# Routing work moved into VectorE's waits, own buffers for the sample's rows, a deeper last stage, two up accumulators

## What is computed

```
x = x + gt1 * (concat(a_out, b_out) @ w_out)      # b_out = y * sigmoid(y @ w_glu + b_glu)
h = rms_norm(x, g_norm2) * (1 + sc2) + sh2        # shift, scale, gate: one row per sequence
g_prob = softmax(h @ w_group + b_group);  g_idx = argmax       # 4 groups
e_logits = h @ w_expert + b_expert                              # 32 experts, 8 in a group
e_top, e_idx = top_2 of the 8 logits in the chosen group
gate = g_w * softmax(e_top)
x = x + gt2 * sum_k gate_k * (silu(h @ w1[e_k]) * (h @ w3[e_k])) @ w2[e_k]
y = rms_norm(x, g_final)
```

## Time and profile before

| | us |
|---|---|
| median of 3 runs | 1870.66 (1867.41 to 1872.51) |
| the profiled execution's own time | 1870.08 |
| its span, first to last instruction | 1868.4 |
| busy in the span: PE, DVE, ACT, POOL | 1449.6, 1007.3, 568.4, 701.0 |

### The profile page before, as it was taken

The page is one execution under the profiler, slowest core; times in us unless marked ns, Lnnn a source line. Parts: engine busy times, 40 slices in busy tenths (PEclk is TensorE's granted clock), DMA queues, the critical chain, the costliest instruction groups (busy, mean ns, idle before and its releaser), DMA issues. The chain is left out here.

```text
span 1868.4 us, 26204 instructions
## 1 busy us (share of the span) xinstructions
PE 1449.6 (78%) x6641; PEld 1086.6 (58%) x6642; DVE 1007.3 (54%) x2144; ACT 568.4 (30%) x976; POOL 701.0 (38%) x545
## 2 busy tenths in 40 slices
PE   3891899999859999398888886189999999994000
PEld 0140688888635666177777775168788887883000
DVE  3993756556355330335445553468555585761567
ACT  1121422323120000211111211068554485661232
POOL 0841223232115320023433333237443365563664
PEclk9996899999965555599999998589999999997555
DMA  4756311111181001634333342489976599985674
GB/s 117 267 181 219 113 68 45 67 57 61 36 164 40 18 6 69 233 115 166 136 135 135 149 149 73 155 276 372 359 270 244 207 370 363 325 313 184 215 276 161
DMA packets 165677, 322.78 MB, mean 173 GB/s; under 512 B 21677, under 2 KB 93421, under 8 KB 164952
## 3 DMA queue, kind: packets, MB, share of 16 engines
q1 hardware_dynamic: 150426, 276.20, 43.1%
q0 software_dynamic: 13664, 45.70, 7.1%
q10 hardware_dynamic: 1536, 0.26, 0.1%
HBM read 235.74 MB, written 86.39 MB: 172 GB/s over the span
## 5 line engine op out<-in xcount | busy, mean ns | idle before, releaser
L2022 POOL TENSOR_TENSOR down_lo<-expert_raw,down_hi (+1 forms) x64 | 157.1, 2476 | 180.9 <-ACT down_hi L2114 180.9
L2161 DVE TENSOR_TENSOR up_lo<-expert_raw,up_hi (+1 forms) x128 | 170.4, 1372 | 21.0 <-ACT up_hi L2109 20.2
L619 PE MATMUL ps_up<-up_hi,xT_hi 128*128 x400 | 161.8, 405 | 4.5 <-DVE up_lo L2161 2.9
L621 PE MATMUL ps_up<-up_hi,xT_lo 128*128 x400 | 157.2, 393 | 0.0
L620 PE MATMUL ps_up<-up_lo,xT_hi 128*128 x400 | 156.6, 392 | 0.0
L2109 ACT ACTIVATE up_hi<-expert_raw (+1 forms) x128 | 125.3, 1057 | 3.5 <-DMA expert_raw<-in_w 1.7
L619 PE MATMUL ps_out<-wout_hi,catT_hi 128*128 128x512 f32 (+1 forms) x272 | 109.0, 401 | 2.7 <-DVE catT_lo L1607 2.7
L621 PE MATMUL ps_out<-wout_hi,catT_lo 128*128 128x512 f32 (+1 forms) x272 | 107.5, 395 | 0.0
L620 PE MATMUL ps_out<-wout_lo,catT_hi 128*128 128x512 f32 (+1 forms) x272 | 107.4, 395 | 0.0
L448 PE MATMUL ps_ada<-wada,cT 128*9 128x512 f32 x192 | 87.7, 615 | 10.9 <-DMA wada<-in_w_ada 5.8
L782 POOL TENSOR_TENSOR v<-v,lng 128x512 f32<-128x512 f32 (+1 forms) x17 | 21.9, 1290 | 194.6 <-DVE v L931 194.6
(11 more groups left out here) (363 smaller groups left out, 3571.4 us busy)
## 6 DMA issues: line engine op xcount, KB each, us to landing
expert_raw<-in_w SPq DMA_DIRECT2D x96, 1024.0 KB
expert_rows<-yo SPq DMA_DIRECT2D x49, 512.0 KB
wada<-in_w_ada SPq DMA_DIRECT2D x12, 2048.0 KB
x<-in_x_prompt SPq DMA_DIRECT2D x32, 512.0 KB, 3.6
expert_rows<-blank SPq DMA_DIRECT2D x31, 512.0 KB, 4.1
x_rows<-x SPq DMA_DIRECT2D x16, 512.0 KB, 2.6
moe_in_rows<-h SPq DMA_DIRECT2D x16, 512.0 KB
x<-x_rows SPq DMA_DIRECT2D x16, 512.0 KB
```

The lines of the kernel that those rows point to most:

```text
L619: pe.matmul(out, left(0, k), right(0, k), start=k == 0, stop=False)
L621: last = pe.matmul(out, left(1, k), right(0, k), start=False, stop=k == n - 1)
L2022: pool.tensor_tensor(down_piece(down_lo, run, m), raw_piece(run, 2, m, 1), down_piece(down_hi, run, m).bitcast(F32), ALU.subtract).then_in ...
L2161: dve.tensor_tensor(up_piece(up_lo, run, m), raw_piece(run, m // 2, m % 2, KD // 2), up_piece(up_hi, run, m).bitcast(F32), ALU.subtract).t ...
```

## The change

1. `mixout`, VectorE: `select(n-1)` now stands in odd steps between `bias_z` and `gated(i,1)`; `ranks(n-2)` in even steps between `low_y` and `gated(i,0)`; `slots(n-2)` in even steps between `bias_z` and `gated(i,1)`. TensorE's `rank` moves to even steps, between `turn_y` and the first half of the projection; GpSimd's `scatter` to even steps, between `gate_y` and the second half of the residual. In step 16 `select(7)` stands ahead of the reciprocal root.
2. `mixout`: the sample's rows have own buffers `gate_s`, `gain_s`, `shift_s`; their 24 DMAs are issued between steps 13 and 14.
3. `experts`: `pU` has two banks, `up_mm` no longer waits for `h_ok`; `turn_hid(b-1)` stands between `turn_x(b+1)` and `up_mm(b)`, and `evac_hid(b-1)` behind `evac_x(b+1)` on ScalarE and VectorE; VectorE's four splits are all ahead of `hidden`.
4. `final`: six buffers; all 17 tiles written out; no index copy; the gather of tile i+4 is issued behind the multiply of tile i and waits for `x_ok >= i-1`; the sample's gate rows have a semaphore of their own, for which only GpSimd waits, in the last step.

The core of the diff:

```diff
@@ mixout, SP
-                    if static and i == TP:
-                        for q in range(NSEQ):
-                            sp.dma_start(gate[q * DSEQ:(q + 1) * DSEQ, :], ...
...
                 prompt_loop(sp, 0, step)
+                for t, c in ((gate_s, 2), (gain_s, 4), (shift_s, 3)):
+                    for q in range(NSEQ):
+                        sp.dma_start(t[q * DSEQ:(q + 1) * DSEQ, :],
+                                     S.ada_d[1 + q:2 + q, c * D:(c + 1) * D].to_broadcast([DSEQ, D])).then_inc(mod_s, 16)
@@ mixout, TensorE
+                    ranked = b == 0 and not (isinstance(n, int) and n < 2)
                     if not last:
                         turn_y(i + 1, n + b, 1 - b)
+                    if ranked:
+                        pe.wait_ge(l_ok, i - 1)
+                        rank(n - 2, 2)
                     project(i, b, 0)
+                    if ranked:
+                        pe.wait_ge(rk_ok, n)
                     if not last:
                         glu(i + 1, n, 0 if first else i - 1)
                     project(i, b, 1)
-                    if b == 1 and not (isinstance(n, int) and n == 0):
-                        pe.wait_ge(z_ok, i + 2)
-                        rank(n - 1, 2)
@@ mixout, GpSimd
                         gate_y(i + 1, n + b, 1 - b)
+                    if ranked:
+                        scatter(n - 2, 2)
                     residual(i, n, b, 1)
+                    if last:
+                        pool.wait_ge(mod_s, 16 * 3 * NSEQ)
...
-                    if b == 1 and not (isinstance(n, int) and n == 0):
-                        scatter(n - 1, 2)
@@ mixout, VectorE
                         low_y(i + 1)
+                    if ranked:
+                        ranks(n - 2, 2)
                     gated(i, 0)
                     if not last:
                         bias_z(i + 1)
+                    if ranked:
+                        slots(n - 2, 2)
+                    if b == 1 and not (isinstance(n, int) and n == 0):
+                        select(n - 1, 2)
                     gated(i, 1)
-                    if b == 1 and not (isinstance(n, int) and n == 0):
-                        ranks(n - 1, 2)
...
                         logits(i - 1, 1 - b)
+                    if last:
+                        select(7, 2)
                     dve.wait_ge(sq_ok, i + 1)
...
-                    if b == 0 and not first:
-                        select(n - 1, 2)
-                    if b == 1 and not (isinstance(n, int) and n == 0):
-                        slots(n - 1, 2)
@@ experts
-        pU = S.psum(st, "ps_up", [P, 512])
+        pU = S.psum(st, "ps_up", [P, 2, 512])
-                    if not (isinstance(b, int) and b == 0):
-                        pe.wait_ge(h_ok, b)
                 def step(b, j, t):          # TensorE
                     turn_x(b + 1, j + (t + 1) // AHEAD, (t + 1) % AHEAD)
+                    turn_hid(b - 1)
                     up_mm(b, t % 2, run_of(b))
                     down_mm(b - 1, run_of(b - 1))
-                    turn_hid(b)
                 def step(b, j, t):          # VectorE
                     evac_x(b + 1, prev)
-                        split_up(run, range(3))
-                    hidden(b)
-                        split_up(run, range(3, 4))
+                    evac_hid(b - 1)
+                    split_next(dve, b, split_up)
+                    hidden(b, t % 2)
                     out(b - 1, AHEAD // 2 * j + (t - 1) // 2, prev)
-                    evac_hid(b)
@@ final
-        NB = 4
+        NB = 6
                 def step(i, n, b):          # GpSimd
-                    if within(i, NB - 1):
-                        if not (isinstance(i, int) and i == 0):
-                            pool.wait_ge(x_ok, i)
-                        gather(i + NB - 1, (b + NB - 1) % NB)
                     pool.wait_ge(two_ok, i + 1)
+                    if i == TP:
+                        pool.wait_ge(samp_in, 16 * NSEQ)
+                    g = gate_s if i == TP else gate
                     pool.tensor_tensor(yg[0:r, b, 1, :], yg[0:r, b, 1, :], g[0:r, :], ALU.mult).then_inc(mul_ok, 1)
+                    if i + AHEAD < NT:
+                        if i + AHEAD >= NB:
+                            pool.wait_ge(x_ok, i + AHEAD - NB + 1)
+                        gather(i + AHEAD)
-                dve.wait_ge(mod_in, 16 * (2 + NSEQ))
+                dve.wait_ge(mod_in, 16 * 2)
```

More of the change, by code:

```diff
@@ L1454, in step @@
                     if not first:
-                        logits(i - 1, NT if last else i + 2, n + b)
+                        logits(i - 1, NT if last else i + 2)
                 def rank(p, n):
@@ L2142, in _ @@
                 split_down(0)
[L2143 to L2144 removed]
+                silu(0, 0)
                 split_up(1)
@@ L2193, in _ @@
                 evac_x(1, 1)
-                hidden(0)
-                evac_hid(0)
+                hidden(0, 0)
                 split_up(1)
@@ L2268, in step @@
                         sp.dma_start(o.y_prompt[0, ds(i * P, P), :], out[:, b, :]).then_inc(o_out[b], 16)
-                    if not isinstance(i, int) or i + NB < NT:
+                    if i + NB < NT:
                         load(i + NB, b)
-                tiles(sp, step)
+                tiles(step)
                 for b in range(NB):
@@ L2318, in _ @@
                 scale(1, 0, 1)
-                tiles(act, step)
+                tiles(step)
             @block.vector
@@ L2341, in norm @@
                     inv_sqrt(dve, c, rstd[0:r, :], ssq[0:r, b:b + 1], 1.0 / D, newton[0:r, 0:1], newton[0:r, 1:2])
-                    if not (isinstance(n, int) and n == 0):
+                    if n > 0:
                         dve.wait_ge(o_out[b], 16 * n)
@@ L2347, in step @@
                 def step(i, n, b):
-                    if within(i, 2):
-                        add_rows(*later(i, n, b, 2))
-                    if within(i, 1):
-                        residual(*later(i, n, b, 1))
+                    if i + 2 < NT:
+                        add_rows(i + 2, (i + 2) // NB, (i + 2) % NB)
+                    if i + 1 < NT:
+                        residual(i + 1, (i + 1) // NB, (i + 1) % NB)
                     norm(i, n, b)
-                dve.wait_ge(mod_in, 16 * (2 + NSEQ))
+                dve.wait_ge(mod_in, 16 * 2)
                 add_rows(0, 0, 0)
@@ L2357, in _ @@
                 residual(0, 0, 0)
-                tiles(dve, step, lambda i: c.at(INV * i))
+                tiles(step)
 _INS = ['x_prompt', 'x_sample', 'state_ssm_re', 'state_ssm_im', 'c_prompt', 'c_sample', 'w_ada', 'b_ada',
```

109 lines of the change are left out of this document (43 added, 66 removed).

## The result

The changed kernel took 1777.53 us (median of 4: 1743.11, 1746.27, 1808.80, 1808.98), the kernel before 1871.28 beside it; forecast were 1796 us, and 1774 to 1822. The ratio given for it, 0.9327 with an interval of 0.9299 to 0.9354, has to be read with one thing in mind: executions of either kernel fall into two groups some 60 us apart, and this ratio compares the changed kernel's lower group with the other's upper one. The median of four lies between its two groups, where no execution lay; that it falls inside the range is luck. Most of the experiments are about this.

The account below looks back on a forecast made before the run. Bounds: TensorE waiting for VectorE's `yT_lo` in `mixout`, TensorE itself in the experts, a GpSimd-VectorE chain in the last stage. 1870.1 us with -47.2 - 9 + 0 - 7.3 - 10.9 = -74.4 gave 1796 us, range 1774 to 1822.

Parts of the forecast that it names:

- The sum's base: Whole kernel: 1870.08 us profiled and 1870.66 median count as one number; changes under 0.3% (5.6 us) cannot be told.
- Parts 1 and 2: `mixout`: `yT_lo` waits go (-36.4), slow GLU matmuls go (-12.8), later even-step residual (+2), sample-row wait shrinks (-9 us).
- Part 2: Last `mixout` step: less waiting for the sample's rows, -9 us (bounds -4 and -12); loads queued behind the DMAs, 0.
- rivals A and B: `mixout`: A, the wait returns through GpSimd, 1820 us, chance 0.12; B, clock stays 0.94, last-stage period 7.6, 1820 us, 0.08.
- Part 3: `experts`: two up accumulators change only order, `hid` in time behind four splits: 0 us, bounds -3 and +10.
- rival D: `experts`: both `down_lo` block VectorE's splits, `hid` 3.7 us late 32 times, 118 us: 1914 us, chance 0.02.
- Part 4: Last stage: first `out_rows` earlier, -7.3 us; period 6.95 instead of 7.63 us, -10.9 us (bounds 0 and -21).
- the hold: Last stage: VectorE's newton step stands until GpSimd's multiply ends, 1.87 us against 0.22, keeping the period at 6.95 us.

Follow-up runs that it names:

- the six matmuls: Six more fp32 128x512 matmuls, result overwritten, ahead of the sums of `s5`'s fifth tile: 1792.11 us in the kernel before, 1723.72 us in the changed one.

## Why the prediction was wrong

- **The sum's base: the step that failed.** "So one number serves both", and "a measurement of this kernel tells no change from one under 0.3%": 1870.08 less the change's terms took for granted that every stage left alone keeps its time. `s5` stood in the sum at nothing and measured -61.8 us in the profiled execution. I read the granted clock of `mixout`, the experts and the last stage, and not that of `s5`, where TensorE stood at 0.50 from 574 to 750 us with no wait. That stage ran in 242 us or, to judge by the totals, shorter in 11 of 49 executions (181 where it rose by itself in a profile, 161 with the six matmuls). The profile before shows its low clock, and not that it would ever rise: the three executions known then all lay in the upper group. So the two groups, 1806 and 1743, could have been a rival, but their shares not. A single range of 48 us could not hold both.
- **Parts 1 and 2** (-56.2): -52.4, -51.1 and, in pairs with the six matmuls, 428.5 - 375.1 = -53.4. The waits for `yT_lo` went, all 36.4 us; the clock went to 0.99. What is missing is the term that Part 2 put at nothing, "what is queued behind them ... still has the rest: 0". The 15.4 us in which SP idles were read from a step of the old length; in the changed kernel it idles 8.1 us there (982.98 to 991.05), and the load of the last `cat` tile, which stands behind the 24 issues, is issued at 1007.62 instead of 999.45. TensorE waits 3.67 us for it and the step loses 6.0; without that, `mixout` would be at -58.4, an estimate. The rivals A and B did not occur: in the even step the residual starts at 899.08 behind the scatter, and `h` and `yT_lo` follow at 903.53 and 904.73 with no idle time of TensorE.
- **Part 3** (0, -3 to +10): +6.3 in the first profile, +5.2 in the means. The step that failed is "`hid` is there at about 1262.6, TensorE wants it at 1262.8". A margin of 0.2 us, taken from one block whose splits ran without a stall, was no margin: 15 blocks lost up to 0.7 us each as "issue", 7.8 in all, and 1.0 in the block shown, all told. And the rest of the part, the second accumulator with the moved `turn_hid`, was costed at nothing, although it was worth -4.8. Two errors of opposite sign looked like a small one. The mechanism is rival D's, at about 1 us in some 15 blocks instead of 3.7 in 32.
- **Part 4** (-18.2): -17.5, by its steps: first `out_rows` 29.8 us behind the first DMA (29.4 forecast), period 6.97 (6.95), newton steps of 1.88 (1.87).
- **In like groups** the change is worth -66.1, -69.4 and -68.4 us against -74.4: 3 to 5 us missing in `mixout`, 5 to 6 in the experts. So the forecast was good for the change, and wrong for what would be measured.

On the hold: the Trainium skill's page "GPSIMD Engine Reference", section "Key points", which names contention of GpSimd with VectorE instructions of two SBUF inputs, is borne out more directly than before, by 1.88 us with GpSimd's multiply and 0.22 without.

## What to carry to other kernels

Read the granted clock of every stage, also of those that the change leaves alone: a stage that is 100% busy at 0.50 may have two durations, as `s5` had, and their difference (62 to 82 us here) is larger than most changes. Before two kernels are compared, force that stage to one level, or compare executions of one group. Where something is there only 0.2 us before it is wanted, count the stall of the neighbour in it. Before transfers are put into a queue's idle time, take that time from the step as it will be, and look at what the next load behind them feeds. And take an operation off the engine that holds another, even if the held engine must do it itself.

## What the runs showed of the hardware

- TensorE can be busy for 176 us without a break (574 to 750 us in the kernel before) at a granted clock of 0.50; in the changed kernel, whose `s5` is the same code, the clock rose at 613 us and stayed at 1.00 to the end of `s5`. What decides between them is not settled: it rose by itself at 613 and 615 us in two profiles (the changed kernel and the one with the changed `mixout` alone) and at times not recorded in other executions (totals of 1775, 1793 and 1845 us lie between the groups). The Trainium skill's page "TensorE: Matmul & The Clock Gate", section "Part 1: The HAM clock gate (the "warmup" mystery)", says that the throttled state is the default and that activity releases it, and that how much of a kernel runs before the release varies from run to run. A variation is seen here too, though a larger one (a rise in `s5` in 11 of 49 executions); that activity is enough does not agree, as long as busy time in the profile's sense is meant: these rows show it busy and throttled.
- Six fp32 matmuls of 128x512 raised it in every profile that had them; one wait of 1.11 us behind the rise was followed by a fall that lasted for the rest of the stage. That it was the wait that did it is argued: eight profiles with waits of 0.30 us at most in the tiles that follow had no fall there, and the one with 3.5 us fell too, but no run makes or takes away the wait alone, and 0 of 18 at the places without one is too few to tell.
- Eight broadcast DMAs of sample rows take SP 2.7 us to issue; 24 of them ahead of a load put that load 8.2 us later, and TensorE stopped 3.67 us for it.
- Where `hid` ended 0.05 us before its reader began, TensorE lost 0.7 us under the name "issue" ahead of the next group. Such rows stand 15 times in the stage (7.8 us), against 2 (0.8 us) where `hid` comes one split earlier. A wait can stand in the profile under another name than that of what is late.
